# Splits, squares and copies reordered between the output product of the cross attention and the first feed-forward slabs

## The reference

```
x = x + rmsnorm(mixed @ w_out, norm_mix_post)                       # mixer block: ssm and window attention
h = rmsnorm(x, norm_x_pre)
x = x + rmsnorm(cross_attention(h, mk, mv, w_xq, w_xo), norm_x_post)  # 4 heads, 256 memory tokens
h = rmsnorm(x, norm_ff_pre)
x = x + rmsnorm(square(relu(h @ w_ff1)) @ w_ff2, norm_ff_post)        # 1024 -> 4096 -> 1024
```

## Time and profile before

| | us |
|---|---|
| median of 3 runs (lowest, highest) | 1316.51 (1314.3, 1316.98) |
| profiled execution | 1312.32 |
| its span | 1310.7 |
| TensorE busy | 1232.0 (94%) |
| VectorE busy | 672.3 (51%) |
| ScalarE busy | 509.9 (39%) |
| GpSimd busy | 274.7 (21%) |
| share of TensorE in the chain that ended last | 88% |

### The profile page before, as it was taken

How to read it: one execution, slowest core, us unless ns; L and a number is a source line. 1 busy time by engine, 2 the same in 40 slices (tenths; PEclk the granted TensorE clock), 3 DMA queues, 4 the chain that set the end, 5 groups by cost and what they waited for, 6 DMA issues and landing times.

```text
span 1310.7 us, 23215 instructions
## 1 busy us (share of the span) xinstructions
PE 1232.0 (94%) x10054; PEld 1149.9 (88%) x10054; DVE 672.3 (51%) x873; ACT 509.9 (39%) x912; POOL 274.7 (21%) x221
## 2 busy tenths in 40 slices
PE   6899999999888899999979988988999999999995
PEld 6799999999777899999979977778989989989974
DVE  5354998997476445543673332364424423423434
ACT  5564444441377634335543332253312312312321
POOL 1067999991100000002450000000000000000012
PEclk9899999999899899999989997998999999999998
DMA  8142213322102434314436210211222222232221
GB/s 219 49 141 66 66 51 94 100 89 91 56 3 84 144 98 115 124 58 129 145 118 204 65 65 17 66 48 58 104 81 65 97 81 69 93 97 59 87 65 72
DMA packets 152723, 115.67 MB, mean 88 GB/s; under 512 B 7056, under 2 KB 134992, under 8 KB 152304
## 3 DMA queue, kind: packets, MB, share of 16 engines
q1 hardware_dynamic: 147552, 106.13, 26.8%
q10 hardware_dynamic: 5072, 8.08, 1.7%
HBM read 102.21 MB, written 12.12 MB: 87 GB/s over the span
## 4 chain that ended last, share of the span: by engine, by line
PE 88%; DVE 5%; ACT 3%; issue 1%; DMA 1%; ACTq 1%; POOL 0%; POOLq 0%; SPq 0%; DVEq 0%
PE gp L1832 37%; PE sp L2261 10%; PE gp L2261 10%; PE gp L2347 9%; PE sp L2347 5%; PE sp L2240 2%; PE sp L1990 2%; DVE wL L1257 1%; PE sp L1984 1%; PE gp L2215 1%; PE sp L1967 1%; PE sp L2319 1%; PE gp L1848 1%; PE gp L2009 1%; DMA gate<-gates_scratch 1%
## 5 line engine op out<-in xcount | busy, mean ns | idle before, releaser
L1257 DVE TENSOR_TENSOR wL<-wraw,wH 128x1024 fp32r<-128x1024 f32 x164 | 216.4, 1323 | 244.4 <-ACT wH L742 243.6
L742 ACT ACTIVATE wH<-wraw 128x1024 fp32r<-128x1024 f32 x164 | 172.8, 1054 | 258.7 <-PE sp L2261 165.0
L1832 PE MATMUL gp<-aH,wH 128*128 128x288 f32 (+2 forms) x928 | 204.5, 302 | 12.8 <-ACT z L837 5.8
L1832 PE MATMUL gp<-aH,wL 128*128 128x288 f32 (+2 forms) x928 | 200.5, 298 | 0.0
L1832 PE MATMUL gp<-aL,wH 128*128 128x288 f32 (+2 forms) x928 | 200.4, 298 | 0.0
L1832 PEld LDWEIGHTS gp<-aH,wH 128*128 128x128 f32 x928 | 152.2, 192 | 17.1 <-issue 15.0
L1832 PEld LDWEIGHTS gp<-aL,wH 128*128 128x128 f32 x928 | 152.6, 192 | 0.0
L1832 PEld LDWEIGHTS gp<-aH,wL 128*128 128x128 f32 x928 | 152.4, 191 | 0.0
L718 POOL TENSOR_TENSOR oT<-oT,gff 128x512 f32<-128x512 f32 x4 | 5.4, 1369 | 596.9 <-ACT dump L1214 596.9
L2261 PE MATMUL gp<-wH,fH 128*128 128x512 f32 x208 | 82.8, 398 | 3.4 <-DVE h0s L1685 2.0
L2261 PE MATMUL gp<-wL,fH 128*128 128x512 f32 x208 | 82.2, 395 | 0.0
(11 more groups left out here) (396 smaller groups left out, 2594.9 us busy)
## 6 DMA issues: line engine op xcount, KB each, us to landing
wraw<-in_w_ff SPq DMA_DIRECT2D x64, 512.0 KB, 3.8
wraw<-in_w_in SPq DMA_DIRECT2D x36, 512.0 KB, 4.3
gates_scratch<-sq ACTq DMA_DIRECT2D x16, 288.0 KB, 2.4
gate<-gates_scratch SPq DMA_DIRECT2D x16, 288.0 KB, 3.9
wraw<-in_p_att SPq DMA_DIRECT2D x8, 512.0 KB, 3.8
wraw<-in_w_glu SPq DMA_DIRECT2D x8, 512.0 KB, 3.7
wraw<-in_p_ssm SPq DMA_DIRECT2D x8, 512.0 KB, 3.6
wraw<-in_w_out SPq DMA_DIRECT2D x8, 512.0 KB, 3.7
```

The source lines that it names most:

```text
L742: s_.activation(wH[s][:], wraw[w][:], ACT.Copy).then_inc(wh_done, 1)
L1257: v.tensor_tensor(wL[s][:], wraw[w][:], wH[s][:], ALU.subtract).then_inc(wl_done, 1)
L1832: last = mm(gp[:, b + h, 0:n], w[:, k, :], y[:, k, c0:c0 + n], start=(k == 0 and w is wH[s] and y is xh), stop=(k == KT - 1 and w is wL[s]))
```

## The change

Five edits, with no other loads, products or buffers:

- ScalarE runs one square root on a constant before the splits of the output product. The table of square roots is loaded there and no longer at the first `out_root`.
- ScalarE and VectorE treat the squares, the copy `h0s` and the gains of the first half's units 0 to 3 before the split of XO+7, not after it. `fold` is made first.
- The split of FF slab 2 stands before the norms of "h" and row 2 on ScalarE, and before `row_xn("h")` on VectorE.
- The split of FF slab 3 stands before the last `x2_root`, and before `row_xn` of row 2.
- TensorE transposes rows 2 and 3 after all four `first_ff1(j, 0)`, not between them; "h" stays where it was.

```diff
--- before.py
+++ after.py
@@ -1177,10 +1177,12 @@
                 s_.activation(bH[:, :, t0:t0 + rows].rearrange("p (b k) q -> p b k q", b=2),
                               ROW_BANKS[u].rearrange("p b (k q) -> p b k q", k=4)[:, :, :, 0:rows], ACT.Copy).then_inc(bh_done, 1)
 
-            for j in range(5):
+            seq(s_.activation(stat(3, 0), eps[:], ACT.Sqrt))
+            for j in range(4):
                 split_h(T_XO + j + AHEAD, j + AHEAD)
             for u in range(4):
                 square_out(0, u, u + 1)
+            split_h(T_XO + 4 + AHEAD, 4 + AHEAD)
             seq(s_.activation(nst[:, 2, 0:4], nst[:, 0, 0:4], ACT.Identity, bias=eps[:, 0:1], scale=1.0 / D))
             split_h(T_FF, 0)
             square_out(0, "h", 5)
@@ -1195,14 +1197,14 @@
             rows_h(0, 1)
             out_root(2, 4)
             rows_h(1, 2)
+            split_h(T_FF + 2, 2)
             x2_root("h", 3)
             x2_root(2, 4)
-            split_h(T_FF + 2, 2)
             out_root(3, 5)
+            split_h(T_FF + 3, 3)
             rows_h("h", 3)
             x2_root(3, 5)
             rows_h(2, 4)
-            split_h(T_FF + 3, 3)
             rows_h(3, 5)
 
             def square_unit(u, c):
@@ -1706,16 +1708,17 @@
                                 ROW_BANKS[u].rearrange("p b (k q) -> p b k q", k=4)[:, :, :, 0:rows],
                                 bH[:, :, t0:t0 + rows].rearrange("p (b k) q -> p b k q", b=2), ALU.subtract).then_inc(bl_done, 1)
 
-            for j in range(5):
-                split_l(T_XO + j + AHEAD, j + AHEAD)
             for h in range(2):
                 last = v.tensor_tensor(fold[:, 64 * h:64 * h + 64], ident[:, 64 * h:64 * h + 64], ident[:, 64 - 64 * h:128 - 64 * h], ALU.add)
             last.then_inc(fold_ready, 1)
+            for j in range(4):
+                split_l(T_XO + j + AHEAD, j + AHEAD)
             dve.wait_ge(xtok_cp, 5)
             half_copy(0)
             dve.wait_ge(g3_loaded, 16)
             for u in range(4):
                 out_gain(0, u)
+            split_l(T_XO + 4 + AHEAD, 4 + AHEAD)
             split_l(T_FF, 0)
             out_gain(0, "h")
             split_l(T_FF + 1, 1)
@@ -1733,13 +1736,13 @@
             rows_l(1, 2)
             row_x2("h", 3)
             row_x2(2, 4)
+            split_l(T_FF + 2, 2)
             row_xn("h", 3)
             out_gain(1, 3)
             row_x2(3, 5)
-            split_l(T_FF + 2, 2)
+            split_l(T_FF + 3, 3)
             row_xn(2, 4)
             rows_l("h", 3)
-            split_l(T_FF + 3, 3)
             row_xn(3, 5)
             rows_l(2, 4)
             rows_l(3, 5)
@@ -2329,8 +2332,10 @@
                 pe.wait_ge(ss0_ready, ss0)
                 pe.wait_ge(ss1_ready, ss1)
                 first_ff1(j, 0)
-                if j:
-                    turn_row(ROWS[j + 1], j + 2)
+                if j == 1:
+                    turn_row("h", 3)
+            turn_row(2, 4)
+            turn_row(3, 5)
             pe.wait_ge(bl_done, 5)
             for j in range(4):
                 first_ff1(j, 1)
```

## The result

The changed kernel's median is 1301.95 us (1299.02 to 1304.08, 4 runs) against 1315.4 us for the kernel before (1314.08 to 1316.98, 4 runs). The ratio is 0.9895, 95% interval 0.9877 to 0.9913: 11.4 to 16.2 us less (13.8 by the ratio, 13.45 between the two medians). The forecast was 1306.5 us with a range of 1302.0 to 1311.5.

What follows compares the result with a forecast made beforehand. TensorE was taken to bound the kernel, losing time ahead of 912.5 us to waits and half clock. Waits of 7.7 us plus 2.3 of clock made 10.0, so 1316.5 - 10.0 = 1306.5 us, range 1302.0 to 1311.5.

Steps and rivals of the forecast that it cites:

- The walk: Step-by-step timing of the engines from the output product to the second token range: 11.2 us less than the profiled execution.
- Part 1: First half's copy and squares in the output product: h0s wait goes, 2.0 us, and the half-clock stretch behind it, 1.6 us.
- Part 2: Feed-forward slabs 2 and 3: earlier splits remove both wL waits and mostly a half-clock stretch; second token range 7.6 us earlier.
- The table load at 0: Square-root table load moved from row 0's chain to the output product's start: hidden there, counted as 0 us.
- The wait of 2.4 us for bL stays: Ahead of the second token range TensorE still waits 2.4 us for bL, as before.
- two thirds of the 3.5 that the walk gives: Clock part of the gain, cut to 2.3 us because idle time need not always bring half clock; total gain 10.0 us.
- I leave one half-clock stretch in the second token range: Second token range: one half-clock stretch remains as before, counted as 0 us.
- Only the waits count: Rival: clock losses stay the same in median on both sides; gain 7.7 us, 1308.8 us, chance 0.22.
- All clock losses go: Rival: all three half-clock stretches vanish along with the waits; gain 12.6 us, 1303.9 us, chance 0.10.
- Late norms: Rival: row norms behind two splits on VectorE come late, or the h0s wait stays; gain 6 to 8, chance 0.15.
- a wait found again: Rival: bL of row 3 sets the second token range's start, so waits return there; gain 0 to 2.6, chance 0.04.
- a clock that stays low for long: Rival: 4.2 us without a product keeps TensorE at 1.2 GHz from the second token range on; 1319 or more, chance 0.03.

Runs made afterwards that it cites:

- e3: Kernel before with only the table load moved to the start of the output product: 1314.01 us against 1314.53, ratio 0.9997.
- e8: Changed kernel without the early square root, so the table load is back in row 0's chain: 1303.51 us, ratio 0.9916 to the kernel before.
- e5: Changed kernel with transposes of rows 2 and 3 back between slabs 2 and 3 and behind 3: 1303.02 us, ratio 0.9914 to the kernel before.
- e4: Changed kernel run again without edit, beside the kernel before: 1301.78 us against 1314.53, ratio 0.9912.
- e7: Kernel before with TensorE's waits for h0s and for wL of slabs 2 and 3 filled with useless products: 1311.48 us against 1314.74, ratio 0.9982.
- e6: Kernel before with eight useless products filling TensorE's wait for h0s: 1312.8 us against 1314.74, ratio 0.9992.
- e1: Kernel before with only the first half's h0s, squares and gains put ahead of the split of XO+7, fold first: 1308.2 us against 1314.53, ratio 0.9956.
- e9: Kernel before with only the split of slab 2 put ahead of the norms: 1311.34 us against 1314.93, ratio 0.9976.
- e10: Changed kernel run a third time without edit, beside the kernel before: 1303.81 us against 1314.93, ratio 0.9913.
- e12: Changed kernel with rows 2 and 3 transposed inside slab 3 and row 1 three products earlier: 1301.22 us, ratio 0.9896 to the kernel before.
- e11: Changed kernel with the transposes of rows 2 and 3 put inside slab 3's first range: 1299.82 us, ratio 0.9887 to the kernel before.

## Why the prediction was too low

**The walk held.** Part 1: the wait of 1.98 us went, nothing took its place, and h0s is ready 4.5 us before TensorE writes its bank. Part 2: the starts were met within 0.4 us, counted from slab 0 (wL of slab 2 at +2.6 where the walk has +2.7, wL of slab 3 at +7.1 against +7.2, xn of row 3 ends at +11.7 against +11.8, second range +17.0 against +16.7). The table load at 0 is shown by e3 and e8. "The wait of 2.4 us for bL stays" is 2.6: the transposes in one piece let bH of row 3 follow bH of row 2, and e5 has 2.4 again. One reading was wrong and did no harm: the earlier trace rows has four lines and five waits, not three lines and four waits; the sum of 11.1 is right.

**The step that failed** is the last one, from the walk to the median: "I take two thirds of the 3.5 that the walk gives, 2.3, because the same idle time must not always be followed by half clock". The walk had 11.2 us, the forecast 10.0. The clock's part was mis-sized, as the traces show in two ways. The stretches between TensorE's marks give 11.2 to 12.5 us in the five traces of the changed kernel and of its forms e5 and e8 (90.3 to 91.6 together against 102.8). Less the waits, 7.4 to 7.7 us, the clock's part is 3.5 to 5.0, where 2.3 was taken; what exceeds 3.8 of it, in the first trace and in e4, is chance at the start of the product or in the second range. And e7, with the waits only filled, has 2.9 us in the trace (0.8 to 4.1 in the median).

The reason given holds for a single wait, not for the place. The stretch behind the wait for h0s is there in four of four traces, and e6 takes it away by filling the wait. Behind the waits for slabs 2 and 3 it moves: at slab 3 in the kernel before and e3, at slab 2 in e6, at both in e1. But each of these four traces has at least one, and slab 0 to second range takes 24.2 us or more in them, and 17.0 in all that have both splits moved and the transposes outside slab 3. "I leave one half-clock stretch in the second token range" was met in four of the five traces; in e4 it was missing, and e1, e6 and e9 show that with the wait of before it can be missing too (14.2 us in place of 15.7). That one is chance.

**What this step doesn't explain.** The forecast was 4.55 us too high, and the discount is 1.2 of that. Another 1.1 us is the starting value: I subtracted from 1316.5, the median of three runs, while the kernel before has 1315.4 in the comparison (and 1314.5 to 1314.9 on the other chips, from 17 to 24 runs). The remaining 2.25 us are what the two medians differ by beyond the walk, 13.45 against 11.2; of these, what the traces don't have stays open. Nor do the medians alone refute the discounted 10.0 us: the first interval (11.4 at least) excludes it, those of e4 and e10 hold it. That the discount was wrong rests on the traces.

**The rivals.** "Only the waits count" (7.7) is outside the interval of the first comparison and of e4 and e10 (8.7 and 8.5 at least). "All clock losses go" (12.6) has a mechanism, that none is left ahead of the second range or in it, that holds in one trace of five. The three ratios give 13.8, 11.6 and 11.4 us: the last two lie nearest to the walk without a discount, 11.2. Late norms, a wait found again, and a clock that stays low for long were not seen. The Trainium skill, TensorE: Matmul & The Clock Gate, section "What's actually happening", which I set beside the discount, speaks of a kernel's start. There the traces agree: over the first 100 us, where the code is the same, the granted clock is 0.93 in the kernel before, 0.91 in the changed one, 0.90 in e1 and 0.95 in e12. What I drew from it for the wait for h0s, that the stretch would be missing in part of the runs, no trace shows.

**What stays open.** The first comparison's 13.8 us is 1.3 us more than the best pair of traces shows. Kernels that are the same up to 800 us begin the output product between 807.3 and 813.8 us, and what makes these 6.5 us isn't known. The medians of the changed kernel lie at 1301.95, 1301.78 and 1303.81. So I can't tell an effect of 1 us from scatter, and the 0.05 us by which the median left the range is such scatter. That the sum was cut by 1.2 us is not.

## What to carry to other kernels

Where one engine is busy without a gap behind the changed place, as TensorE is here, its waits add up one for one: list them and walk the other engines' lists with durations from the rows. Here such a walk was right within 0.4 us. Price an idle TensorE with what its clock does behind it, and don't discount that for chance before more than one trace has been looked at. Take the starting value from more than three runs, where runs scatter by more than the terms you argue about. Filling the wait with useless products into a bank that is written anew prices the clock alone. A last chain of transposes, copy and rest is shortened by giving it the tail of the product ahead of it, as e11 does.

## What the runs showed of the hardware

An idle time of 1.98 us was followed by 3.4 us at the 1.2 GHz level in four of four traces, and the wait of 2.41 us ahead of slab 2 by none in the first trace and in e3, but by one in e1 and e6. I had not expected the shorter wait to be the dependable one. In e1, where the first wait was gone and all else stood 3.6 us earlier, counted from the start of the output product, the half clock came at 879 to 886, around the wait of 2.4 us, so that slab 0 to second range took 26.8 us, 2.5 more than before: removing one idle time moved where the next ones cost. Over all three stretches that trace gained 2.7 us, not 3.6.
